# Level-1 inverse matrices from PSUM, and the end of the RWKV recurrence merged with the output projection

## The reference

```python
def step(state, inp):                       # wkv7, per head of 64
    r_t, w_t, k_t, v_t, z_t, b_t = inp
    sa = einsum('bhvk,bhk->bhv', state, z_t)
    state = (state * w_t[:, :, None, :] + sa[..., None] * b_t[:, :, None, :]
             + v_t[..., None] * k_t[:, :, None, :])
    return state, einsum('bhvk,bhk->bhv', state, r_t)
...
mean = y.mean(-1); var = ((y - mean) ** 2).mean(-1)          # per head
y = ((y - mean) * rsqrt(var + GN_EPS)) * ln_w + ln_b
y_a = (y + bonus) * g
y_b = h * gelu(bg)                                           # RG-LRU half
x = x + concatenate([y_a, y_b], -1) @ w_out
```

## Time and profile before

| | us |
|---|---|
| median of 3 runs | 2730.03 |
| lowest, highest | 2727.56, 2731.19 |
| the profiled execution | 2726.26 |
| its span | 2724.5 |

### The profile page before, as it was taken

How to read it: one execution, slowest core, us unless ns; L and a number is a source line. 1 busy time by engine, 2 the same in 40 slices (tenths; PEclk the granted TensorE clock), 3 DMA queues, 4 the chain that set the end, 5 groups by cost and what they waited for, 6 DMA issues and landing times.

```text
span 2724.5 us, 35571 instructions
## 1 busy us (share of the span) xinstructions
PE 2593.1 (95%) x13471; PEld 2160.4 (79%) x13471; DVE 1307.9 (48%) x1580; ACT 921.8 (34%) x1404; POOL 878.2 (32%) x790
## 2 busy tenths in 40 slices
PE   6999789999699999999999999989999999999998
PEld 4778578787587887888788888978878888888886
DVE  5532277777434556474564445642344414431443
ACT  3442344453423322343243334522232213321333
POOL 4222244444322224585572221112222222222221
PEclk7999899999899999999999999989999999999999
DMA  2111000000012211242251124631111111111112
GB/s 89 45 45 46 24 1 1 1 1 1 17 47 62 55 47 54 67 161 89 68 176 58 45 93 164 209 93 49 48 43 50 47 50 46 46 50 50 46 47 85
DMA packets 239924, 164.58 MB, mean 60 GB/s; under 512 B 23981, under 2 KB 227271, under 8 KB 237767
## 3 DMA queue, kind: packets, MB, share of 16 engines
q1 hardware_dynamic: 224960, 141.10, 17.2%
q10 hardware_dynamic: 14855, 22.01, 2.3%
HBM read 129.51 MB, written 29.36 MB: 58 GB/s over the span
## 4 chain that ended last, share of the span: by engine, by line
PE 63%; issue 4%; DVE 2%; POOL 2%; ACT 1%; DMA 0%; SPq 0%; POOLq 0%; DVEq 0%; ACTq 0%
PE acc_o L1562 53%; PE acc_o L1811 3%; PE bank_a L2756 1%; POOL dense_lo L374 1%; PE bank_b L2779 1%; PE acc_o L2111 1%; PE bank_b L2464 1%; PE bank_b L2469 1%; PE bank_a L2455 1%; POOL c_lo L2616 0%; DVE val L2044 0%; PE bank_b L2768 0%; PE bank_b L2769 0%; PE bank_b L2767 0%; POOL t_gx L2387 0%
## 5 line engine op out<-in xcount | busy, mean ns | idle before, releaser
L374 POOL TENSOR_TENSOR dense_lo<-dense_raw,dense_hi 128x512 fp32r<-128x512 f32 (+2 forms) x318 | 419.5, 1320 | 1154.0 <-ACT dense_hi L367 1152.8
L367 ACT CAST dense_hi<-dense_raw 128x512 fp32r<-128x512 f32 (+2 forms) x318 | 188.6, 594 | 750.8 <-PE acc_o L1562 705.5
L1562 PE MATMUL acc_o<-a_hi,dense_hi 128*128 128x512 f32 x1304 | 405.1, 392 | 5.6 <-POOL dense_lo L374 3.4
L1562 PE MATMUL acc_o<-a_lo,dense_hi 128*128 128x512 f32 x1304 | 402.8, 390 | 0.0
L1562 PE MATMUL acc_o<-a_hi,dense_lo 128*128 128x512 f32 x1304 | 402.0, 389 | 0.0
L1562 PE MATMUL acc_o<-c_hi,dense_hi 128*128 128x512 f32 x1096 | 340.7, 392 | 23.4 <-POOL dense_lo L374 21.8
L1562 PE MATMUL acc_o<-c_lo,dense_hi 128*128 128x512 f32 x1096 | 338.7, 390 | 0.0
L1562 PE MATMUL acc_o<-c_hi,dense_lo 128*128 128x512 f32 x1096 | 338.5, 390 | 0.0
L1562 PEld LDWEIGHTS acc_o<-a_hi,dense_hi 128*128 128x128 f32 x1304 | 242.3, 188 | 57.6 <-issue 3.6
L1562 PEld LDWEIGHTS acc_o<-a_hi,dense_lo 128*128 128x128 f32 x1304 | 245.2, 188 | 51.6
L1562 PEld LDWEIGHTS acc_o<-a_lo,dense_hi 128*128 128x128 f32 x1304 | 245.2, 188 | 51.5
(11 more groups left out here) (392 smaller groups left out, 3752.1 us busy)
## 6 DMA issues: line engine op xcount, KB each, us to landing
dense_raw<-in_f_w_up SPq DMA_DIRECT2D x176, 256.0 KB, 3.0
dense_raw<-in_f_w_down SPq DMA_DIRECT2D x72, 256.0 KB, 2.9
w_raw_e<-in_e_w_in SPq DMA_DIRECT2D x44, 256.0 KB, 2.9
s_states<-t_hx ACTq DMA_DIRECT2D x16, 512.0 KB, 3.0
g_in<-s_inputs SPq DMA_DIRECT2D x8, 1024.0 KB, 5.1
hx<-s_states SPq DMA_DIRECT2D x8, 1024.0 KB, 5.2
dense_raw<-in_o_w_glu SPq DMA_DIRECT2D x32, 256.0 KB, 2.8
s_inputs<-t_in ACTq DMA_DIRECT2D x14, 512.0 KB, 2.7
```

Source lines behind the costliest of these rows:

```text
L367: nc.scalar.copy(self.hi[:, par, 0:n, :], self.raw[:, par, 0:n, :]).then_inc(w_hi_done, 1)
L374: pool.tensor_tensor(self.lo[:, par, 0:n, :], self.raw[:, par, 0:n, :], self.hi[:, par, 0:n, :].bitcast(F32), op=ALU.subtract).then_inc(w_ ...
L1562: last = nc.tensor.matmul(acc[:, h * HALF:(h + 1) * HALF], w[:, chunk, j, :], x[:, k + j, h * HALF:(h + 1) * HALF], start=first, stop=final)
```

## The change

Two parts of the program change.

*In each chunk.* "first" is no longer made from a_b (SBUF) in one operation per g after n = 1, but from the score banks in PSUM, two parts per g: after n = 0 and after n = 1, each for two of the four matrices. As the banks of n = 1 are now read twice, scores n = 3 wait for "first" as well. The codes of the next chunk move from behind scores n = 3 to ahead of it.

*At the end.* The group norm of the last chunk leaves the recurrence's block and goes into the next one. y_tiles begins with the LRU tiles 14 to 17; the projection's first two units are written out in OUT_PLACES order: LRU half of unit 0, LRU half of unit 1, RWKV half of unit 0, RWKV half of unit 1. The first two weight chunks are loaded by SP already in the recurrence's block, once x_t of the last chunk is made; dense_raw, head_ones, centre and unscale get fixed addresses for that. The LRU tiles 0, 2, 3 get their c_hi on VectorE, and all c_lo are made by VectorE. The steps of out_pool for this chunk are done by VectorE.

```diff
@@ scores_pe
             if n == 3:
                 wait(pe, "a_kept", c, 4)
+                wait(pe, "first", c, 4)
@@ scores_dve
-                if n == 1:
+                if n < 2:
                     for g in range(2):
-                        wait(dve, "a_kept", c, 3 + g)
                         wait(dve, f"res_ps{g}", c, 2, back=1)
-                        up(tt(mx[g][:, :, :], a_b[g][:, :, 0, :],
-                              level_mask[:, 0, :].unsqueeze(1).to_broadcast([P, RT, CH]), ALU.mult), "first")
+                        up(tt(mx[g][:, 2 * n:2 * n + 2, :],
+                              score_banks[n][g].rearrange("p (i a t) -> p i a t", i=2, a=2)[:, :, 0, :],
+                              level_mask[:, 0, :].unsqueeze(1).to_broadcast([P, 2, CH]), ALU.mult), "first")
@@ turn_of_pe
-            for n in (1, 2, 3):
+            for n in (1, 2):
                 scores_pe(pe, c, s, n)
             if more:
                 lora_codes_pe(pe, c + 1)
+            scores_pe(pe, c, s, 3)
             level0_pe(pe, c)
@@ the recurrence's block: SP, and what leaves the other engines
+                for g in range(2):
+                    wait(sp, f"x_t{g}", last_chunk)
+                for n in range(2):
+                    load_out(sp, dense_raw, n, 0, n)
...
-                centred_act(act, last_chunk, True)
-                logs_act(act, last_chunk + 2, 1, 1)
-                roots_act(act, last_chunk + 2, 1, 1)
...
-                y_floor_dve(dve, last_chunk)
-                gn_dve(dve, last_chunk)
...
-                out_pool(pool, last_chunk)
...
-                centre_pe(pe, last_chunk)
-                y_sum_pe(pe, last_chunk)
@@ the next block, TensorE
+                last_centre_pe(pe)
+                out_products(pe, 0, 0, 1)
+                last_sum_pe(pe)
+                out_products(pe, 0, 1, KC)
+                out_products(pe, 1, 0, KC)
+                out_products(pe, 2, KC, DT)
+                out_products(pe, 3, KC, DT)
-                with pe.Fori(0, DT // 2) as i:
+                with pe.Fori(1, DT // 2) as i:
@@ ScalarE
+                dn.take_hi(act, DT, u_out, 0, 0, 1)
+                y_hi_act(act, 1)
+                last_centred_act(act)
+                dn.take_hi(act, DT, u_out, 0, 1, 2)
+                last_roots_act(act)
+                dn.take_hi(act, DT, u_out + 1, 0, 0, 1)
+                wait(act, "out", last_chunk, RT + 2)
+                for k in range(4, DT):
+                    y_hi_act(act, k)
+                dn.take_hi(act, DT, u_out + 1, 0, 1, 2)
@@ VectorE
+                y_part(dve, 0)
+                y_part(dve, 1)
+                last_floor_dve(dve)
+                y_part(dve, 2)
+                y_part(dve, 3)
+                last_out_dve(dve)
+                for k in range(4, DT):
+                    y_part(dve, k)
```

More of the change, by code:

```diff
@@ L1318, in first_pool @@
             for g in range(2):
[L1319 removed]
+                wait(pool, "first", c, 3 + g)
                 wait(pool, f"x_t{g}", c, back=1)
@@ new lines, in trunk, with out_products @@
+        OUT_PLACES = ((0, 0), (1, 0), (0, 1), (1, 1))
+        def out_products(pe, n, first, end):
+            unit, chunk = OUT_PLACES[n]
+            if not chunk and first == 0:
+                pe.wait_ge(unit_free, u_out + unit + 1)
+            pe.wait_ge(w_lo_done, 2 * u_out + n + 3)
+            for k in range(first, end):
+                last = tile_products(dn, pe, DT, c_hi, c_lo, unit, k, y_ready, n % 2, dn.acc[unit])
+            if end % KC == 0:
+                last.then_inc(w_used, 1)
```

111 lines of the change are left out of this document (74 added, 37 removed).

## The result

| | before | after |
|---|---|---|
| median of 4 runs, us | 2728.80 | 2700.17 |
| lowest, highest | 2727.01, 2731.19 | 2697.96, 2701.21 |
| the profiled execution, its span | 2726.26, 2724.5 | 2697.96, 2696.2 |

A forecast was written before the change was run, and what follows sets the result against it. The prediction took TensorE, busy 95% of the span, as the bound, with VectorE limiting each chunk's front. Gains of 10.6 us (chunk fronts) and 16.0 us (end) gave 2730.03 - 26.6 = 2703.4 us, range 2698 to 2712.

The forecast's parts named there:

- The parts of "first": Chunk front, VectorE: four PSUM parts at 0.38 us each, making "first" complete about 2.2 us earlier.
- The new wait for sig_g: Chunk front: TensorE waits 0.95 us for ScalarE's sig_g before the codes, replacing a 0.55 us wait.
- The 1.27: Chunk front: x_inv[1] starts 1.27 us sooner in each of seven chunks, 8.9 us in all.
- The last chunk: Recurrence's final chunk, without codes: level-1 mask 1.7 us sooner; 1 to 2 us more from the clock not counted.
- The end: Merged group norm and output projection: unit 1 done at 748.9 instead of 764.88, gaining 16.0 us, bounds 13 to 17.8.
- The copy that might lock GpSimd out: End: by a skill rule, VectorE's SBUF cast would block GpSimd's weight work, costing up to 0.8 us more.
- (b): Chunk front gives nothing, through the sig_g wait or another hidden limit; 2712.3 us, chance 0.06.
- (d): Slower: the 0.95 us gap makes the clock fall in each chunk, with a slow end; 2750 us, chance 0.03.
- (e): End: early products held by weights or the block's end, saving only some 8 us there; 2711.4 us, chance 0.05.
- (a): End gives less: TensorE's low clock holds through tile 3 and unit 1; 11 us gained there, 2708.4 us, chance 0.14.
- (c): More gain: the clock falls neither in the last chunk nor at the end; 29.9 us off, 2700.1 us, chance 0.10.
- part 1: Chunk fronts: "first" from PSUM in four parts and codes ahead of scores n=3; 10.6 us off, bounds 8 to 12.

The follow-up runs named there:

- late_parts: The changed kernel with all four parts of "first" made behind the masks of n=1, none ahead of them; 2700.29 us, ratio 0.9905.
- sum_first: The changed kernel with the sum product for the last variance ahead of the products of tile 0; 2696.50 us, ratio 0.9887.
- codes_only: The kernel before with only the next chunk's codes moved ahead of scores n=3, "first" still from a_b; 2727.91 us, ratio 1.0005.

## Why the prediction was right

The forecast was 3.2 us too high, inside its range. The places of the gain and the waits that went were right; one term, the last chunk, was less than half of what came, and two errors at the end cancelled. The stretches give 1.7 of it: 1.1 from the chunks, 2.4 from the last chunk, 0.4 from the end, less 1.9 of scatter ahead of the recurrence and 0.4 of the rest. The 1.9 and the last 0.4 are luck, being within the scatter of those stretches. The other 1.5 comes from the frame: I put the median 3.77 above the profiled execution, and in the changed kernel it is 2.21 above.

- **The parts of "first"** took 414 ns, two of them 0.74 from start to end, against 0.38 each. The complete "first" is there 2.3 us earlier, against 2.2.
- **The new wait for sig_g** is 0.95 us, as worked out. In the old frame the codes start at 628.21 (628.2), scores n=3 at 629.21 (629.3), level 0 at 630.17 (630.2), x_inv[1] at 631.66 (631.8), the mask at 633.46 (633.6). The period is 46.20 against 46.3. The 1.27 became 1.40, mostly as level 0 took 1.45 and not 1.55.
- **The last chunk** is the term that was mis-sized: 1.7 predicted, 4.14 measured. Its front gave 1.99 (first closing products 8.58 us behind the turn of k_t, where they were 10.57), near the 1.7. The other 2.15, behind those products, is the clock that no longer falls, which the prediction named ("that would give 1 to 2 us more. I do not count it") and left out.
- **The end** gave 16.4 against 16.0, in part by two errors that cancel. Tile 3 started 12.43 us behind the copy of y and not 11.37, 1.05 late: the low clock came earlier than I had put it, at tile 0 and the sum product (2.69 us for a tile that takes 1.36), and lay in the chain sum, floor, tiles 2 and 3, gn. The prediction had both ends for tile 0, 723.6 and 725.1, and put the floor "at about 725.5", which fits the first alone. In late_parts, where the clock held, tile 3 started at 11.06. From tile 3 to the residual sum it then took 18.06 at the full clock, where I had 19.45 with 1.75 for a low one. That the two meet within 0.4 us is luck. Tile 0 itself was right, 4.08 behind the copy against 4.17, the cast 0.69 against 0.75.
- **Not foreseen at the end:** GpSimd's two weight subtractions beside VectorE's two took 4.58 us, and VectorE's last two sums took 2.55 beside a third (from 720.60), where sum_first has 1.42. In sum_first the two engines meet as well, but there VectorE's second sum began first, and GpSimd's subtraction took 1.71 instead of 1.29. Each time the later of the two paid. Hence the output is ready 16.7 us behind the copy and not 14.3. It cost nothing: the first c_lo of the RWKV half is ready at about 724.8, and TensorE comes to it at 725.12. The "ready before TensorE comes" held by 0.3 us only.
- **The copy that might lock GpSimd out** decided nothing: VectorE's cast ended at 707.31, and GpSimd started at 707.34, as soon as its weights had been cast (707.26). The two never met, so this place does not test that rule. The two-input operations behind it collided. The 2.49 us that the prediction quotes for a subtraction "beside GpSimd" is a mean with one that ran alone in 1.23; the three beside GpSimd took 2.9 each. It changed nothing in the sum.
- **Three numbers contradicted the working:** gn "at 728.2 to 729.3" by the chain, where 725.1 and 4.6 make 729.7; some 3.5 us to the first product where the sum had 4.17, and gn 10.5 us behind the copy where it had 11.4. The trace has 4.08 and 12.30; the worked-out ones were nearer.

Of the rivals, (b), (d) and (e) are out: the period fell, the clock is full in each chunk, and the end is 16.4 us shorter. Rival (a) is out too: TensorE was slow at tile 0, from 709.8 to 712.5, and at the full clock from tile 3 (718.15) through unit 1. Rival (c), with 2700.1, has nearly the measured time, but half of its mechanism: the clock held in the last chunk and fell at the end. (In late_parts it held at both, and the end took 29.09, which is the prediction's bound without a fall, 46.85 - 17.8.) That the number agrees to 0.1 us is luck.

The reason given for part 1 was incomplete. "First" did get cheaper by the amount read from the rows, but as a collision that ended, not as a cheaper operand. The forecast did not depend on that; the choice of the edit does, since one wait on GpSimd gives 1.68 a chunk where the rewriting gives 1.40.

## What to carry to other kernels

Where a VectorE operation with both inputs in SBUF takes twice what its shape takes elsewhere, look at what GpSimd does beside it before rewriting it: one wait on GpSimd took 1571 ns to 683, and here was worth as much as reading from PSUM. Work moved ahead to fill a wait paid nothing while the engine that sets the stretch was unchanged (codes_only), and a short product that starts a long chain did better ahead of the bulk products in TensorE's queue (sum_first, 2.4 us). When a clock drop of the profile before stands in the changed stretch, give it a term with a chance of its own; leaving it out was the largest miss here.

## What was unexpected of the hardware

- The size of the contention: 1571 ns for 683 on VectorE, and on GpSimd 2.95 for two that take 2.50 to 2.53 without it; at the end 4.58 for two beside two VectorE operations of 128x1024.
- VectorE casts 128x1024 from SBUF to fp32r in 0.69 us, where ScalarE takes 1.04. The Trainium skill, "VectorE: DVE Perf Modes", section "The perf-mode tier table (the rule you actually need)", gives 1227 ns for a float32 copy of 2048 elements within SBUF. The trace is near it: 0.69 us for half of them, 56% of that time.
- The clock of the last chunk, 0.66 or 0.83 in five profiles and 1.00 in nine: with about the same idle time in the front in one of either kind (2.2 and 2.4 us), and 0.66 and 0.83 behind two fronts with the same waits. At the end it fell in all kernels but late_parts, whose end has the same instructions as that of the changed kernel.
- The stretch ahead of the recurrence, the same instructions in all kernels, takes 337.8 to 341.2 us from one execution to the next, and the rest behind unit 1 1956.6 to 1964.7: either is more than most single edits here are worth.
